# The inverse root of the norms: columns from the sums on, a repeated column in place of diagonals

## What is computed

```
def rms_norm(x, g):
    xf = x.astype(jnp.float32)
    y = xf * lax.rsqrt(jnp.mean(xf * xf, axis=-1, keepdims=True) + RMS_EPS)
    return (y * g.astype(jnp.float32)).astype(x.dtype)
...
def hybrid_layer(x, ...):                       # twice
    hn = rms_norm(x, norm_g[0])
    ... projections, three sparse attentions and a stick-breaking one, merge ...
    x = x + rms_norm(mixed, norm_g[1])
    hf = rms_norm(x, norm_g[2])
    ff = jnp.square(jax.nn.relu(hf @ w_ff1)) @ w_ff2
    return x + rms_norm(ff, norm_g[3])
...
# second network, two blocks: latent attention, then gated linear attention,
# each as x = x + m2 * rms_norm(mixer(modulate(rms_norm(x)))), then
#         x = x + m5 * rms_norm(mlp(modulate(rms_norm(x))))
```

## The kernel before

| line | what |
|---|---|
| L204 | filler of `keep_busy` |
| L236, L269 | squares |
| L245 | root of one row |
| L261, L293, L319 | sums on TensorE (`pe_add`, `pe_add_cols`, `pe_sum`) |
| L280 | addition of squares on VectorE |
| L337, L344 | column matmuls, row matmuls |
| L355, L358 | reciprocal, diagonals |

## Time and profile before

### The profile page before, as it was taken

One profiled execution on the slowest core, in us unless ns is written; L12 is line 12 of the kernel. 1 busy time (PEld: TensorE's weight loads), 2 busy tenths in 40 slices (PEclk: granted clock), 3 DMA queues, 4 the chain that ended last, 5 costly groups with the idle time before them and its releaser, 6 DMA issues. The chain is left out here.

```text
span 3645.6 us, 46669 instructions
## 1 busy us (share of the span) xinstructions
PE 3450.7 (95%) x17972; PEld 2851.2 (78%) x17972; DVE 1940.6 (53%) x2402; ACT 1360.0 (37%) x1991; POOL 561.3 (15%) x394
## 2 busy tenths in 40 slices
PE   6989999999998999999998999899999999999998
PEld 5766878888776687788876888788888788868886
DVE  4264348777526433877765652533333656654444
ACT  3266234444326623444433443312212344432222
POOL 0042004333104200333320110100000100000000
PEclk9999999999998999999998999999999999999999
DMA  3201234443220032344410001111111011112231
GB/s 127 84 1 58 93 105 145 157 158 115 88 84 1 35 105 93 131 158 160 150 52 18 18 12 70 47 58 65 62 59 68 24 68 52 55 35 93 92 102 60
DMA packets 59364, 287.77 MB, mean 79 GB/s; under 512 B 10704, under 2 KB 11984, under 8 KB 31952
## 3 DMA queue, kind: packets, MB, share of 16 engines
q1 hardware_dynamic: 59216, 285.77, 22.7%
HBM read 283.64 MB, written 2.10 MB: 78 GB/s over the span
## 5 line engine op out<-in xcount | busy, mean ns | idle before, releaser
L162 PE MATMUL ps<-h_hi,w_hi_rest 128*128 128x512 f32 (+1 forms) x1072 | 385.2, 359 | 4.6 <-DVE h_lo L386 4.6
L163 PE MATMUL ps<-h_lo,w_hi_rest 128*128 128x512 f32 (+1 forms) x1072 | 363.4, 354 | 0.0
L1343 POOL TENSOR_TENSOR ada_context<-ada_context,ada_scaled 128x768 f32<-128x768 f32 x112 | 287.5, 2567 | 455.2 <-ACT ada_scaled L1425 450.0
L165 PE MATMUL ps<-h_hi,w_lo_rest 128*128 128x512 f32 (+1 forms) x1072 | 322.0, 355 | 0.0
L151 DVE TENSOR_TENSOR w_lo_mix<-w_raw,w_hi_mix 128x2048 fp32r<-128x2048 f32 x94 | 217.1, 2309 | 185.4 <-ACT w_hi_mix L145 185.4
L425 POOL TENSOR_TENSOR x<-x,y 128x512 f32<-128x512 f32 (+1 forms) x32 | 64.5, 2016 | 1522.3 <-DVE y L431 1522.3
L162 PE MATMUL ps<-h_hi,w_hi_mix 128*128 128x512 f32 x736 | 287.0, 390 | 4.5 <-DVE w_lo_mix L151 2.3
L163 PE MATMUL ps<-h_lo,w_hi_mix 128*128 128x512 f32 x736 | 286.5, 389 | 0.0
L165 PE MATMUL ps<-h_hi,w_lo_mix 128*128 128x512 f32 x736 | 286.5, 389 | 0.0
L1507 DVE TENSOR_TENSOR y<-ps,y 128x512 f32<-128x512 f32 (+1 forms) x224 | 165.7, 751 | 216.1 <-PE ps L165 215.3
L145 ACT ACTIVATE w_hi_rest<-w_raw 128x2048 fp32r<-128x2048 f32 x81 | 154.5, 1908 | 326.7 <-PE ps L165 315.5
(11 more groups left out here) (397 smaller groups left out, 7739.6 us busy)
## 6 DMA issues: line engine op xcount, KB each, us to landing
w_raw<-in_stream SPq DMA_DIRECT2D x205, 1024.0 KB, 5.0
ada_raw<-in_ada_w SPq DMA_DIRECT2D x128, 384.0 KB, 5.1
cmp_w<-in_cmp_w SPq DMA_DIRECT2D x8, 1024.0 KB, 7.3
mla_raw<-in_stream SPq DMA_DIRECT2D x8, 512.0 KB, 3.7
x<-in_x SPq DMA_DIRECT2D x1, 2048.0 KB, 8.9
out<-x SPq DMA_DIRECT2D x1, 2048.0 KB, 7.3
x<-in_ctx SPq DMA_DIRECT2D x1, 1024.0 KB, 11.1
consts<-in_consts SPq DMA_DIRECT2D x1, 768.0 KB, 11.7
```

The costliest lines, as they stand in the source:

```text
L162: pe.matmul(out, whi, xhi, start=start, stop=False)
L163: pe.matmul(out, whi, xlo, start=False, stop=False)
L165: last = pe.matmul(out, wlo, xhi, start=False, stop=stop)
L1343: pool.tensor_tensor(ada.context, ada.context, ada.scaled[:, j % 2, :], ALU.add).then_inc(m["context"], 1)
```

## The change

Three things change in `Norm`.
- Where squares are added on VectorE (`pe_sum`), the sum over partitions is taken with `k.acc` as weights and one column of ones as the moving operand, so that it comes out as columns in `stat`. The root is then taken on these nt columns (`act_root_columns`, into a new small tile `root_cols`), and the reciprocal reads it. The one-row root and `pe_columns` fall away there, and `pe_spread_columns` has five fillers in place of four and two.
- Everywhere, `pe_rows` takes as weights one column of `nst` repeated 128 times and as moving operand the identity, and the diagonals fall away.
- The norm `kv` of `stage_values` adds its two squares on VectorE (`dve_gather`, ahead of the products L1849) and takes the new way. Its column matmuls between the tiles fall away.

In `stage_mlp` with `ada`, TensorE waits for the last `take_rows` before `pe_sum`, since both use the same bank, and ScalarE does this `take_rows` before the last square.

```
+    def act_root_columns(self, act):
+        act.wait_ge(self.summed, self.adds * (self.it + 1))
+        act.activation(self.k.root_cols[:, 0:self.nt], self.stat, ACT.Sqrt,
+                       bias=self.k.c["eps"][:, 0:1]).then_inc(self.column, 1)
...
         pe.wait_ge(self.gathered, self.kt - 3)
         keep_busy(pe, k, 3 * self.nt // 2, 1 if self.tok == SEQ else 3)
+        self.pe_column_sums(pe)
+
+    def pe_column_sums(self, pe):
+        k = self.k
         pe.wait_ge(self.gathered, self.kt - 1)
-        for c0, w in chunks(self.tok):
-            last = pe.matmul(self.sums[:, c0:c0 + w], k.c["ones"], k.acc[:, c0:c0 + w], start=True, stop=True)
+        for j in range(self.nt):
+            last = pe.matmul(self.stat[:, j:j + 1], k.acc[:, j * P:(j + 1) * P], k.c["ones"][:, 0:1], start=True, stop=True)
         last.then_inc(self.summed, self.adds)
...
+    def pe_spread_columns(self, pe):
+        keep_busy(pe, self.k, 5 * self.pause, self.free)
         self.pe_rows(pe)
...
     def pe_rows(self, pe):
+        pe.wait_ge(self.inverse, 1 + self.it)
         for j in range(self.nt):
-            pe.wait_ge(self.diag, j + 1 + self.nt * self.it)
-            last = pe.matmul(self.rb[:, j * P:(j + 1) * P], self.k.c["ones"], self.k.diag[:, j * P:(j + 1) * P],
+            last = pe.matmul(self.rb[:, j * P:(j + 1) * P], self.nst[:, j:j + 1].to_broadcast([P, P]), self.k.c["ident"],
                              start=True, stop=True)
...
-    def dve_inverse(self, dve):
-        k = self.k
+    def dve_inverse(self, dve, roots=None):
         dve.wait_ge(self.column, 1 + self.it)
-        dve.reciprocal(self.nst[:, 0:self.nt], self.stat).then_inc(self.inverse, 1)
-        dve.wait_ge(self.inverse, 1 + self.it)
-        for j in range(self.nt):
-            dve.tensor_scalar(k.diag[:, j * P:(j + 1) * P], k.c["ident"], self.nst[:, j:j + 1], None,
-                              ALU.mult).then_inc(self.diag, 1)
+        dve.reciprocal(self.nst[:, 0:self.nt], self.stat if roots is None else roots[:, 0:self.nt]).then_inc(self.inverse, 1)
... stage_mlp, stage_residual, stage_rope_tables: pe_spread, act_root, dve_all
... become pe_spread_columns, act_root_columns, dve_all(dve, k.root_cols)
                 if last_group:
+                    if ada:
+                        pe.wait_ge(m["out"], FF_GROUPS)
                     y_norm.pe_sum(pe)
...
             for t in range(KT):
+                if ada and t == KT - 1:
+                    take_rows(FF_GROUPS - 1)
                 act.wait_ge(s["added"], T2 * (FF_GROUPS - 1) + t + 1)
                 y_norm.act_square_behind(act, t)
-            if ada:
-                take_rows(FF_GROUPS - 1)
... stage_values, TensorE
             keep_busy(pe, k, 5, 0)
-            kv.pe_add(pe, 0)
-            kv.pe_add(pe, 1)
+            kv.pe_column_sums(pe)
             unit_ready(pe, k, n0)
-            values(0, 1)
-            kv.pe_columns(pe)
-            values(1, 3)
+            values(0, 3)
             pe.wait_ge(kv.inverse, 1)
... stage_values, ScalarE: kv.act_root -> kv.act_root_columns; VectorE
+            kv.dve_gather(dve, 1)
             for i in range(2):
                 dve.wait_ge(raw_hi, i + 1)
                 dve.scalar_tensor_tensor(b.raw_lo[:, i, :], ckv[:, i, :], b.g_kv[:, i:i + 1], b.raw_hi[:, i, :].bitcast(F32),
                                          ALU.mult, ALU.subtract).then_inc(raw_lo, 1)
-            kv.dve_inverse(dve)
+            kv.dve_inverse(dve, k.root_cols)
```

More of the change, by code:

```diff
@@ L207 @@
 class Norm:
-    NAMES = ("squared", "summed", "root", "column", "inverse", "diag", "spread", "gathered")
+    NAMES = ("squared", "summed", "root", "column", "inverse", "spread", "gathered")
     def __init__(self, k, name, src, kt, tok, bank, it=0, sems=None, adds=None):
@@ L223, in __init__ @@
         self.sems = sems or [k.sem(f"{name}_{s}") for s in self.NAMES]
-        self.squared, self.summed, self.root, self.column, self.inverse, self.diag, self.spread, self.gathered = self.sems
+        self.squared, self.summed, self.root, self.column, self.inverse, self.spread, self.gathered = self.sems
         self.sums = self.rb = k.ps[:, bank * 512:bank * 512 + tok]
@@ L332, in pe_spread @@
         self.pe_rows(pe)
+    def pe_spread_columns(self, pe):
+        keep_busy(pe, self.k, 5 * self.pause, self.free)
+        self.pe_rows(pe)
     def pe_columns(self, pe):
@@ L341, in pe_rows, with dve_all @@
     def pe_rows(self, pe):
+        pe.wait_ge(self.inverse, 1 + self.it)
         for j in range(self.nt):
-            pe.wait_ge(self.diag, j + 1 + self.nt * self.it)
-            last = pe.matmul(self.rb[:, j * P:(j + 1) * P], self.k.c["ones"], self.k.diag[:, j * P:(j + 1) * P],
+            last = pe.matmul(self.rb[:, j * P:(j + 1) * P], self.nst[:, j:j + 1].to_broadcast([P, P]), self.k.c["ident"],
                              start=True, stop=True)
         last.then_inc(self.spread, 1)
-    def dve_all(self, dve):
-        self.dve_inverse(dve)
+    def dve_all(self, dve, roots=None):
+        self.dve_inverse(dve, roots)
         dve.wait_ge(self.spread, 1 + self.it)
-    def dve_inverse(self, dve):
-        k = self.k
+    def dve_inverse(self, dve, roots=None):
         dve.wait_ge(self.column, 1 + self.it)
-        dve.reciprocal(self.nst[:, 0:self.nt], self.stat).then_inc(self.inverse, 1)
-        dve.wait_ge(self.inverse, 1 + self.it)
-        for j in range(self.nt):
-            dve.tensor_scalar(k.diag[:, j * P:(j + 1) * P], k.c["ident"], self.nst[:, j:j + 1], None,
-                              ALU.mult).then_inc(self.diag, 1)
+        dve.reciprocal(self.nst[:, 0:self.nt], self.stat if roots is None else roots[:, 0:self.nt]).then_inc(self.inverse, 1)
 class Normed:
@@ L1349, in _ @@
             else:
-                n_post.pe_spread(pe)
+                n_post.pe_spread_columns(pe)
             n_pre.pe_all(pe, 9)
@@ L1415, in _ @@
             else:
-                n_post.act_root(act)
+                n_post.act_root_columns(act)
             n_pre.act_all(act, res.wait)
@@ L1463, in _ @@
             for t in range(KT):
+                if ada and t == KT - 1:
+                    take_rows(FF_GROUPS - 1)
                 act.wait_ge(s["added"], T2 * (FF_GROUPS - 1) + t + 1)
                 y_norm.act_square_behind(act, t)
-            if ada:
-                take_rows(FF_GROUPS - 1)
         @block.vector
         def _(dve):
-            n_post.dve_all(dve)
+            n_post.dve_all(dve, None if post_norm is None else k.root_cols)
             res.dve(dve)
@@ L1534, in _ @@
         def _(pe):
-            norm.pe_spread(pe)
+            norm.pe_spread_columns(pe)
             if next_unit is not None:
@@ L1544, in _ @@
                 act.wait_ge(reset, 1)
-            norm.act_root(act)
+            norm.act_root_columns(act)
             if next_unit is not None:
@@ L1554, in _ @@
                 dve.wait_ge(reset, 1)
-            norm.dve_all(dve)
+            norm.dve_all(dve, k.root_cols)
             res.dve(dve)
@@ L1817, in _ @@
                 act.activation(b.raw_hi[:, i, :], ckv[:, i, :], ACT.Copy, scale=b.g_kv[:, i:i + 1]).then_inc(raw_hi, 1)
-            kv.act_root(act)
+            kv.act_root_columns(act)
             for t in range(2):
@@ L2860, in build @@
         k.nst, k.root = at("norm_stat", [P, 8], F32, 59), k.acc[0:1, :]
+        k.root_cols = at("norm_roots", [P, 8], F32, 59.0625)
         k.tiny = at("tiny", [P, 1], F32, 207.75)
```

## The result

The changed kernel took 3623.75 us (median of 8 runs, 3618.09 to 3633.61), the kernel before beside it 3648.27 (8 runs, 3640.68 to 3650.1): ratio 0.9944, 95% interval 0.9934 to 0.9954. The profiled execution took 3626.38 us with a span of 3624.6.

What follows compares the result with a forecast made beforehand. TensorE's matmul stream, busy 95% of the span, was taken as the bound; shortened norm chains gave 15.3 + 0.4 + 1.3 + 2.2 = 19.2 us, less 4.5 for the clock: 3649.6 - 14.7 = 3635 us, range 3628 to 3643.

Steps and rivals of the forecast that it cites:

- The sums' length: Norms summed as columns: eight one-column passes take 1.05 us instead of 1.10, 0.05 us gained per norm, 0.4 in all.
- the cover by fillers: Between sums and rows of kind A: five fillers (1.20 us at full clock) outlast root and reciprocal, which cost nothing.
- `o_norm`: Its four turns: matmul tiles already cover the stretch between reciprocal and rows, so the change gains nothing.
- the ff norms' moved wait: Both `ff_norm`: TensorE's new wait for ScalarE's modulation copy costs nothing; uncovered, 0.16 us twice.
- the price of the repeated column: Weight loads of the rows: one column read 128 times was costed the same as a diagonal, no added time.
- kind A: Eight norms with `pe_sum` then `pe_spread`, losing the one-row root and column matmuls: together 15.3 us gained.
- kind B: Eight norms whose squares are added on TensorE, losing only diagonals: 0.16 us each, 1.3 us in all.
- Sum 2.2, bounds 0 and 3.8: `stage_values`: 1.0 us from TensorE's shorter order plus 1.2 from six diagonals VectorE loses.
- I charge a third, 4.5 us: Seven exposed kind A norms: clock falls would cost 13.4 us if at all, nothing if none; a third charged.
- The sum's reference: Starting time from which the forecast gain of 14.7 us was taken: 3649.6 us, the median of the runs shown.
- Rival 1: The clock holds at all seven exposed norms, so the gain is 19.2 us and the time 3630.4; chance 0.31.

Runs made afterwards that it cites:

- e4: Changed kernel with column sums that move 128 columns a pass instead of one, root reading every 128th column; 3624.4 us, ratio 0.9937.
- e2: Kernel before with only the rows' weights as a repeated column and no diagonals; old sums and root kept; 3642.19 us, ratio 0.9991.
- e8: Changed kernel with 128-column sums, three more fillers ahead of the last addition's wait, and three fillers for five before the rows; 3619.49 us, ratio 0.9923.
- e10: Repeat of e4: changed kernel with column sums moving 128 columns; 3621.87 us, ratio 0.993.
- e6: Changed kernel, one-column sums, with three fillers in place of five between sums and rows; 3622.36 us, ratio 0.9938.
- e11: Repeat of e8: 128-column sums, filled wait, three fillers before the rows; 3619.09 us, ratio 0.992.
- e15: Changed kernel, one-column sums, with three more fillers ahead of the wait for the last addition; 3620.27 us, ratio 0.9927.
- e16: e15 put off by twelve more filler matmuls at the first norm; 3628.1 us, one run.
- e13: Changed kernel, one-column sums, delayed by twelve more filler matmuls ahead of the first norm's fillers; 3625.97 us, ratio 0.995.
- e14: Changed kernel with 128-column sums, delayed by twelve more filler matmuls at the first norm; 3624.75 us, ratio 0.9945.
- e9: Kernel before with twelve more filler matmuls ahead of the first norm's columns, a pure delay; 3646.65 us, ratio 0.9999.
- e1: The changed kernel again, no edit, for a second profile; 3622.66 us, ratio 0.993.
- e3: Changed kernel with the norm kv of `stage_values` summed the old way on TensorE, column matmuls after tile 0; 3623.79 us, ratio 0.9936.
- e12: As e8 but with two fillers in place of three before the rows; 3618.79 us, ratio 0.9918.

## Why the prediction came out as it did

**Right.** The sums' length (1.05 us forecast and measured), the cover by fillers, `o_norm`, the ff norms' moved wait (the stretch before ff of layer 2 is 0.2 us shorter, not longer) and the price of the repeated column. The norms of kind A at full clock measured 3 x 1.62 + 2 x 1.69 + 2.13 + 2.08 + 3.47 = 15.9 us for 15.3 (the 2.08 of mlp0 is from e4, since it was low with all one-column sums; the 3.47 of mla is at the lower level, as forecast), kind B 1.8 for 1.3.

**Mis-sized: `stage_values`, "Sum 2.2, bounds 0 and 3.8".** It measured 2.4 and 1.34, together 3.8, the upper bound itself. I had taken 1.0 of the range 1.2 to 2.6 for TensorE's order because the long L1849 showed VectorE held up, and because the clock might rise later. VectorE is held up, each product now 2.5 us, but the addition ran at 1.03 us in time when VectorE had nothing to do; I had let it delay the products by up to 1.4 us. And the clock stayed at 0.50 for 6.8 us of the piece, as before. Without that the 1.0 would have been right (1.1, e2 against e8). The rule of the Trainium skill (GPSIMD Engine Reference, section 1 Specifications) on the shared interface would, as I read it, have put the addition near 2.3 us. GpSimd's L1808 and L1809 ran beside it, and it still took 1.03; the rule speaks for the products (5.06 us for two), and not for this one.

So at an unchanged clock the change is worth 15.9 + 0.4 + 1.8 + 3.8 = 21.9 us, where I had 19.2. Executions with the same mean granted clock bear this out: at 0.982 the kernel before has a mean of 3646.6 us (26 executions) and the changed one 3625.1 (4), 21.5 less; at 0.983 it is 3641.0 (7) and 3620.2 (5), 20.8 less; at 0.980 3650.3 (4) and 3627.7 (2), 22.6 less.

**Wrong: "I charge a third, 4.5 us".** The mechanism is there. Four of seven norms were low in the profile after, where I had written two or three, at a cost of 1.46 + 1.34 + 0.62 + 1.63 = 5.05 us, close to the charge; the 1.34 belongs to the stretch that began before its norm, so the agreement is in part luck. What failed is to charge it to the whole on top of the time at 0.50 that the kernel before had. Taken from the mean clock of each execution, twice what is missing to 1.00 by the span, the time at 0.50 is 132 us (error 1.0) in the 57 executions of the kernel before that have their clock on record and 133 (3.2) in 13 of the changed one: no more. What appeared at the norms of the first profile was missing in the attention stretches. Single profiles scatter: 119.7 to 148.6 us with old sums, 128.2 to 155.1 with one-column sums and the wait, 124.8 and 125.0 with the wait filled, 125.0 to 132.4 with wide ones. Whether the changed kernel would be faster without falls is not clear at five fillers (e4 and e10: 1.1 us, error 1.6) and likely at three (e6 against e8 and e11: 4.3, error 1.9).

**The sum's reference.** I set it against 3649.6 us, the median of three runs. The 65 runs of the kernel before beside the result and the experiments have a median of 3647.5 and reach from 3635.7 to 3652.2. Two microseconds of the miss are this.

The miss is thus 3635.0 - 3623.75 = 11.25 us: 4.5 of the charge, 2.7 of sizes, 2.1 of the reference, and some 2 that I can't place; the mean of 13 runs of the changed kernel has a standard error of 1.3, and by the means of all runs (3646.4 and 3624.0) the change is worth 22.4 us. Rival 1 came nearest with its number, 3630.4, but not by its condition, for the clock did not hold at all seven places.

The Trainium skill, TensorE: Matmul & The Clock Gate, section "HAM oscillation — how this bites in real kernels", blames idle gaps for the fall. The runs bear it out in small part. With the gap filled, six of seven norms had no fall (e15, e16), but e13 had none at these six with the gap unfilled. Wide sums behind the unchanged gap of 0.93 us had none at all seven (e10, e14), and neither had the old sums behind the same gap. So gaps alone don't tell the kernels apart here, and what the passes move matters too.

**Open:** what decides which form an attention stretch takes. In layer 1 it had 34.1 us at 0.50 in eight profiles and 37.6 to 44.4 in the other ten, and before, profiled twice, was in both groups. In layer 2 both profiles of before had 44.4 and all sixteen others less (30.7 to 41.0), e9 with its old norms among them (37.6); so I can't exclude that the new norms favour the short form there. The state of the clock before each stretch wasn't varied by itself. Open is also why a low stretch that begins among the group matmuls lasts longer with one-column sums behind it.

## What to carry to other kernels

Cost the shortened chain at the clock that the trace shows (in `stage_values` the same change of order was worth 2.4 us at the lower level and 1.1 at the full one), and take a fall of the clock at one place off the total only if the whole's time at the lower level rises with it. For that use the mean clock of many executions and not one profile: at an equal mean clock the two kernels differ by 20.8 to 22.6 us, while the runs of either reach over 15 us. Where a new instruction goes into time in which its engine waited, cost only what sticks out, and take the row of its own shape. When fillers cover a chain that has become shorter, shorten them too (five to two with wide sums, some 4 us more, 3618.79 us). Let column sums move 128 columns: they cost 0.1 us more each, no norm fell with them, and with three fillers the whole was 4.3 us faster (error 1.9) for it and for the filled wait together.

## What the hardware showed unexpectedly

- A weight load from one column read 128 times takes as long as from 128 columns (190 against 192 ns in the middle).
- Passes that move one column take nearly as long as passes that move 128 (eight weight loads 0.97 us both ways, 1.35 against 1.45 us up to the next filler), but only with the one-column ones was the granted clock at 0.50 between sums and rows (18 of 49 norms against 0 of 49; in 3 of the 18 it had fallen 8.8 us ahead of the sums).
- Identical instructions took 495.7 to 501.2 us in layer 1's attention, mostly by how much of it ran at 0.50 (34.1 to 44.4 us), in programs that differ in a few microseconds ahead of it.
- A low stretch in the group matmuls of a layer began 8.8 to 10.1 us ahead of the norm's sums in six of the profiles (after, e1, e2, e3, e11, e12), with old, one-column and wide sums alike.
